# Summing the modulation partials with a two-column matmul instead of a transpose and a VectorE reduction

## The reference, cut to what matters

```
def _modulation(cond, w, b):
    m = jax.nn.silu(cond) @ w + b            # (1, 1024) @ (1024, 6144) + (6144,)
    return tuple(mi[:, None, :] for mi in jnp.split(m, N_ADA, axis=-1))
...
mod_ctx = _modulation(c_ctx[None, :], w_ada[l], b_ada[l])
mod_lat = _modulation(c, w_ada[l], b_ada[l])
```

## Time and profile before

| what | value |
|---|---|
| median of 3 runs | 1533.67 us (1531.07 to 1534.62) |
| the profiled execution: its time | 1531.07 us |
| its span, first to last instruction | 1529.2 us |
| mean granted TensorE clock | 0.995 |
| TensorE matmul busy | 1476.6 us (97%) |
| VectorE busy | 1111.9 us (73%) |
| ScalarE busy | 922.4 us (60%) |

### The profile page before, as it was taken

The page is one execution under the profiler, slowest core; times in us unless marked ns, Lnnn a source line. Parts: engine busy times, 40 slices in busy tenths (PEclk is TensorE's granted clock), DMA queues, the critical chain, the costliest instruction groups (busy, mean ns, idle before and its releaser), DMA issues.

```text
span 1529.2 us, 19534 instructions
## 1 busy us (share of the span) xinstructions
PE 1476.6 (97%) x7393; PEld 1183.8 (77%) x7393; DVE 1111.9 (73%) x1719; ACT 922.4 (60%) x1178; POOL 181.8 (12%) x220
## 2 busy tenths in 40 slices
PE   5999999999998999999999999999999899999997
PEld 3689866669886888888869988666899678888885
DVE  4447657774647999999873665767564699999986
ACT  1323569981225877778752355999412478788774
POOL 0100012200121000000140000221004110000002
PEclk9999999999999999999999999999999999999999
DMA  9555432216538999999855644112431899999993
GB/s 350 177 192 205 157 116 91 90 59 219 214 145 331 364 404 408 409 406 409 319 198 174 215 170 167 64 64 69 158 112 54 330 361 409 413 411 408 404 355 125
DMA packets 132420, 371.96 MB, mean 243 GB/s; under 512 B 9184, under 2 KB 12640, under 8 KB 132320
## 3 DMA queue, kind: packets, MB, share of 16 engines
q1 hardware_dynamic: 113728, 326.57, 56.8%
q0 software_dynamic: 10144, 24.13, 4.4%
q10 hardware_dynamic: 8448, 19.94, 3.3%
HBM read 350.66 MB, written 19.94 MB: 242 GB/s over the span
## 4 chain that ended last, share of the span: by engine, by line
PE 83%; DVE 6%; ACT 4%; DMA 3%; issue 3%; POOL 1%; SPq 0%; POOLq 0%; DVEq 0%; ACTq 0%
PE bank L561 24%; PE bank L915 21%; PE bank L921 11%; PE bank L550 10%; PE bank L571 3%; DMA ring<-in_w_ada 2%; PE bank L766 2%; PE bank L887 2%; PE bank L739 1%; PE bank L594 1%; PE bank L676 1%; PE bank L671 1%; PE bank L958 1%; PE bank L1023 1%; PE bank L866 1%
## 5 line engine op out<-in xcount | busy, mean ns | idle before, releaser
L1975 DVE TENSOR_TENSOR spot_low<-spot,piece_high 128x2048 fp32r<-128x2048 f32 x192 | 433.7, 2287 | 33.1 <-ACT piece_high L1334 32.1
L1334 ACT ACTIVATE piece_high<-spot 128x2048 fp32r<-128x2048 f32 x192 | 366.7, 1917 | 44.9 <-PE bank L921 42.7
L915 PE MATMUL bank<-piece_high,ga_r 128*128 128x512 f32 x768 | 308.7, 402 | 2.9 <-DVE spot_low L1975 1.6
L915 PE MATMUL bank<-spot_low,ga_r 128*128 128x512 f32 x768 | 301.7, 393 | 0.0
L921 PE MATMUL bank<-piece_high,ga_r 128*128 128x512 f32 x768 | 211.0, 396 | 3.7 <-DVE ga_r L1981 3.7
L561 PE MATMUL bank<-parts_r,ga_r 128*128 128x384 f32 x768 | 202.6, 345 | 0.0
L550 PE MATMUL bank<-hT,ring 128*128 128x384 f32 x544 | 185.0, 494 | 4.4 <-ACT ga L1272 2.3
L921 PEld LDWEIGHTS bank<-piece_high,ga_r 128*128 128x128 f32 x768 | 144.0, 188 | 39.2 <-DVE ga_r L1981 5.0
L915 PEld LDWEIGHTS bank<-piece_high,ga_r 128*128 128x128 f32 x768 | 144.3, 188 | 36.2 <-DVE spot_low L1975 2.6
L915 PEld LDWEIGHTS bank<-spot_low,ga_r 128*128 128x128 f32 x768 | 144.6, 188 | 30.6
L550 PEld LDWEIGHTS bank<-hT,ring 128*128 128x128 f32 x544 | 102.1, 193 | 71.2 <-ACT ga L1272 3.1
(11 more groups left out here) (336 smaller groups left out, 2307.8 us busy)
## 6 DMA issues: line engine op xcount, KB each, us to landing
spot<-in_w_gate_up SPq DMA_DIRECT2D x128, 1024.0 KB, 8.0
spot<-in_w_down SPq DMA_DIRECT2D x64, 1024.0 KB, 7.9
ring<-in_w_ada SPq DMA_DIRECT2D x24, 2048.0 KB, 8.0
ring<-in_w_in SPq DMA_DIRECT2D x22, 2048.0 KB, 7.9
expert_rows<-gb ACTq DMA_DIRECT2D x28, 512.0 KB, 7.2
ring<-in_w_attn_proj SPq DMA_DIRECT2D x4, 2048.0 KB, 7.9
ring<-in_w_rnn_proj SPq DMA_DIRECT2D x4, 2048.0 KB, 12.8
ring<-in_w_out SPq DMA_DIRECT2D x4, 2048.0 KB, 8.4
```

Source lines behind the costliest of these rows:

```text
L915: pe.matmul(out[n], high[:, 2 * q + k, :], w[:, k, n * 512:(n + 1) * 512], start=(q == 0 and k == 0 and i == 0), stop=False)
L1334: ac.activation(highs[p % HIGHS], spots[u], ACT.Copy).then_inc(S("piece_high"), 1)
L1975: ve.tensor_tensor(spots_low[u], spots[u], highs[p % HIGHS].bitcast(F32), ALU.subtract)\
```

## The change

In `mod_sum` and `late_mod_sum` the four transposes become four ordinary fp32 matmuls. The block of `ada_part(cc)` stays the stationary operand, 128x128. The moving operand is `sumsel`, 128x2, a constant that has ones in column 0 on the partitions 0, 32, 64, 96 and in column 1 on the partitions 1, 33, 65, 97. So each matmul turns a block and sums its four groups in one, into two columns of the bank. In `mods_added` the reduction is gone, and two additions, one for each stream, read the bank's eight columns and the bias and write `modT`. They don't wait for each other. `sumsel` is already among the loaded constants.

```diff
@@ mod_sum
                 for j in range(4):
-                    mm = pe.transpose(bank[:, j * P:(j + 1) * P], ada_part(cc)[:, j * P:(j + 1) * P], ident)
+                    mm = pe.matmul(bank[:, 2 * j:2 * j + 2], ada_part(cc)[:, j * P:(j + 1) * P], sumsel,
+                                   start=(j == 0), stop=(j == 3), skip_group_check=True)
                 mm.then_inc(S("tran_done"), 1)
@@ mods_added
                 b = v_ada(l, cc * 4, cc * 4 + 4)
+                pair = bank[:, 0:8].rearrange("p (j s) -> p j s", s=2)
+                ve.tensor_tensor(modT[:, cc * 4:cc * 4 + 4, 0], pair[:, :, 0], b, ALU.add)
+                ve.tensor_tensor(modT[:, cc * 4:cc * 4 + 4, 1], pair[:, :, 1], b, ALU.add)\
+                    .then_inc(read, 1)
                 kk = 4 * (cc % 2)
                 m = modT[:, cc * 4:cc * 4 + 4, :]
-                groups = bank.rearrange("p (j g r) -> p j r g", j=4, g=4)[:, :, 0:2, :]
-                link(ve.tensor_reduce(m, groups, AX.X, ALU.add))
-                ve.tensor_tensor(m, m, b.rearrange("p (j a) -> p j a", a=1).broadcast_to([P, 4, 2]), ALU.add)\
-                    .then_inc(read, 1)
```

## The result

| | median, us | runs |
|---|---|---|
| the kernel before | 1533.67 | 7, from 1531.07 to 1534.62 |
| the changed kernel | 1542.09 | 7, from 1538.92 to 1546.27 |

The ratio is 1.0057, with an interval of 1.0042 to 1.0074. That is +8.8 us by the ratio (+8.4 between the medians), where +7.1 was forecast. Run again later as a kernel of its own, the changed kernel gave 1539.87 against 1532.11, a ratio of 1.0047 [1.0031, 1.0062], which is +7.2 us. The profiled execution took 1542.47 us for a span of 1540.7 us, at a mean granted clock of 0.992.

What follows compares the result with a forecast made beforehand. TensorE was taken to bound the kernel. Fourteen stream sums +6.4, chunks 8 +0.6, start +0.25, chunks 7 +0.1 and the late pair -0.3 give +7.1 us: 1533.67 becomes 1540.8 us, range 1536.5 to 1545.5.

Steps and rivals of the forecast that it cites:

- The bound: TensorE, busy for 97% of the span, sets the time; TensorE time added in the streams should come out at the end.
- The rival that hides the q, xr and attention stages: Unseen waits there absorb the added records, so only six sums in the projections' stages count: +2.8 us; chance 0.09.
- Two records a call, each with its own load: In each sum, an ordinary fp32 matmul is two records, each loading 128 columns, so four calls become eight records.
- The price: Eight records of 0.113 us take 0.90 against 0.44 for four transposes: +0.46 us for each sum in a stream.
- The page beside it: The skill's load rule, 107 ns per 128 columns, estimates 0.85 us for eight records and +0.41 per sum.
- The rival by which a narrow operand is cheap: Two moving columns make each record 0.015 us, so eight take 0.12 and the kernel gains 6.0 us; chance 0.05.
- The dear record: Leaving an fp32r stream for narrow fp32 matmuls costs 0.14 us a record: +11.5 us in all; chance 0.06.
- Where the streams are: Fourteen sums in streams cost +0.46 us each; chunk 8 costs +0.31 and chunk 7 +0.05 in each layer.
- One figure: Layer 0 would be shifted by about 1.9 us by the end of its attention stage.
- VectorE's pair: Two additions starting 0.10 us apart end after 0.27 instead of 0.40, saving 0.13 where the chain passes VectorE.
- The late pair: Chunks 2 and 3 of layer 1, in the first expert: VectorE saves 2 x 0.13, so -0.3 us.
- The start: Only chunk 3 of layer 0 counts, +0.25 us; weight loads hide the three sums before it.

Runs made afterwards that it cites:

- wide: The changed kernel with the 128-column identity as moving operand in place of two columns, VectorE keeping its reduction: 1540.18 us, ratio 1.0055 to the kernel before.
- again: The changed kernel unaltered, run later as a kernel of its own: 1539.87 us, ratio 1.0047 to the kernel before.
- start_only: The kernel before with the new form only for chunks 0 to 3 of layer 0: 1533.86 us, ratio 1.0004.
- base: The kernel before, unaltered, run as a kernel of its own: 1531.99 us, ratio 0.9993.
- rest_only: The kernel before with the new form for all chunks except 0 to 3 of layer 0: 1541.28 us, ratio 1.0044.
- twice: The changed kernel with each of the four narrow matmuls issued two times: 1563.62 us, ratio 1.0196 to the kernel before.

## Why the prediction was right, point by point

- **The bound.** Right: a term that lengthens TensorE's stream in any of the three kinds of stage comes out at the end. The rival that hides the q, xr and attention stages (+2.8 us) falls with the table of stages: the q and xr stages alone grew by 1.3 and 1.4 us, and the chunks 7 to 9 cost another 0.5 in layer 0 (below).
- **Two records a call, each with its own load.** Right: 160 records for 20 sums.
- **The price.** Forecast 0.113 us a record and +0.46 a sum; measured 0.10 and +0.45. The level was a little high on both sides, because the chain adds 0.09 us to the old form too (0.44 there, 0.35 from start to start). The difference, which is what counts, was right. That the load of 128 columns sets this pace, and not something else of a record, is still a reading: wide rules out the moving width, and L779's records with 32 stationary columns are quick, but no run changes the stationary width of a sum.
- **The page beside it.** The Trainium skill ("TensorE: Matmul & The Clock Gate", section "LDWEIGHTS (loading the stationary operand)") gives 107 ns for a load of 128 columns, an estimated 0.85 us for eight. The trace has 0.80 from start to start and 0.90 in the chain with its follower's share, so the spacing agrees, as the prediction said. A load's own record doesn't: it is 192 ns long for 128 columns and 111 ns for L779's 32, and neighbouring ones overlap.
- **The rival by which a narrow operand is cheap** (-6.0 us) falls by wide against again: 0.81 and 0.80 us for eight records. **The dear record** (0.14 us) falls too: sixteen of them take 1.68 us in the middle of an fp32r stream.
- **Where the streams are.** The changed kernel's starts of L580 in the attention stage of layer 0, in TensorE's order of time:

```profile
156.89 0.95 PE L580 MATMUL bank<-con,tmp 128*128 128x2 f32 x8
...
182.71 0.95 PE L580 MATMUL bank<-con,tmp 128*128 128x2 f32 x8
...
208.96 0.95 PE L580 MATMUL bank<-con,tmp 128*128 128x2 f32 x8
```

  The kernel before has them at 154.64, 180.46 and 206.50 us. From chunk 7 to 8 it is 25.82 in both: +0.00 for chunk 7, forecast +0.05. From 8 to 9 it is 26.25 and 26.04: +0.21, forecast +0.31. From 9 to 10 (at 355.21 and 352.42) it is 146.25 and 145.92: +0.33, forecast +0.46. So each came out a little under its forecast. TensorE has small waits in the attention stage; that they take up a part is likely, but not shown. All stages behind the start have 6.4 us where these terms gave 7.1.
- **One figure didn't follow from its terms.** The prediction had layer 0 shifted by about 1.9 us at the end of its attention stage. Its own terms for the chunks 4 to 9 give 3 x 0.46 + 0.05 + 0.31 + 0.46 = 2.2. Measured from the start of the q stage to chunk 10 it was 1.9 (2.79 less 0.9). The sum used the terms, not this figure.
- **VectorE's pair** was mis-sized. The changed kernel at the late pair:

```profile
495.57 0.69 DVE L1996 SCALAR_TENSOR_TENSOR gr<-gr,bank 128x512 f32<-128x512 f32 x1
496.18 0.15 DVE L1565 TENSOR_TENSOR modT<-bank,vec 128x4 f32<-128x4 f32 x1
496.25 0.15 DVE L1566 TENSOR_TENSOR modT<-bank,vec 128x4 f32<-128x4 f32 x1
...
497.62 1.22 DVE L1983 TENSOR_TENSOR ga_r<-bank,ga_r 128x1024 fp32r<-128x1024 f32 x1
```

  The additions start 0.07 us apart, not 0.10, and the pair is over in 0.22, where it was expected to take 0.27 and the old one took 0.40. That would account for half of what chunk 8 cost less than forecast (0.21 for 0.31).
- **The late pair** was right. From the last product before it (L1996 above) to L1983 it is 2.05 us. Before, it was 2.35, from the row below to 493.53: -0.30, as forecast, since sixteen records more lay under other work.

```profile
491.18 0.69 DVE L1994 SCALAR_TENSOR_TENSOR gr<-gr,bank 128x512 f32<-128x512 f32 x1
```

- **The start** was forecast at +0.25 us, from durations at the full clock and with chunk 3 alone in the chain. start_only measured +0.6 [-0.9, +2.0], so its size isn't known to better than a microsecond or so, but the traces point to more than 0.25. In again two sums of the start stand in the chain, at the lower clock level, with 1.87 and 1.88 us. The kv weights begin at 43.0, 45.5 and 45.4 us in the three profiles with the narrow form there (the changed kernel, again, start_only), and at 41.8, 42.3 and 43.3 in the three with the old one (the kernel before, base, rest_only). The mean clock over all executions is 0.9936 in again and 0.9957 in wide, against 0.9946 in the kernel before on their chip, and 0.9935 in both start_only and rest_only, against 0.9940 on theirs. Since rest_only has the old form at the start, whether the narrow form itself lowers the clock there stays open.

Together: 6.4 in the stages, -0.3 at the late pair and somewhere between nothing and 2 us at the start are 6 to 8 us. The later comparison's +7.2 [4.7, 9.5] and the first one's +8.8 [6.4, 11.3] both hold that, and the forecast. The late pair's part was read from VectorE's order of time, since the experts of layer 0 around it take between 319.8 and 322.7 us whatever the form (319.9 and 321.8 in two profiles of the kernel before). That the total came so near to 7.1 is in part luck: the streams cost 0.7 us less than their terms, and the start probably more than its own.

## What to carry to other kernels

Where TensorE sets the time, count its records, and not the moving columns of narrow ones (2 and 128 cost the same here): a transpose replaced by an ordinary fp32 matmul on the same block doubles the records, whatever it saves on the other engine. A saving on VectorE counts only where the chain goes through it, here at a few of the 24 sums. Before carrying a price from another line, look at the distance between two starts at the place itself.

## What was not expected of the hardware

Long runs of narrow matmuls can cost more than their time. In twice the granted clock fell to half within a stream that was busy without a gap, at the end of or behind 32 records in a row with 2 moving columns (0.62 in one stretch, 0.51 in another). With 128 moving columns in the sums and the same loads it stayed at 1.00. The stages around the two dips parted by 3.2 us. Shorter runs did nothing of the kind in the middle of the program: neither the seventeen sums of sixteen records in twice, nor the changed kernel's eight with L779's sixteen in front, nor its late pair, sixteen in a row from 494.89 us on; its granted clock from 60 to 760 us, which hold ten of its sums and the late pair, is 1.00. This rests on one trace of each kernel. Why the clock fell with 2 moving columns and not with 128, no run here shows.
